# Down products that read their 512 weight columns from two halves in turns

## The reference

```python
u = jax.nn.relu(jnp.einsum('bsd,df->bsf', h2, w_up[l]))
x = x + jnp.einsum('bsf,fd->bsd', u * u, w_down[l])
...
return jnp.einsum('phk,phkd->pd', (gb * hid).astype(xb.dtype), v_tab[eb])
```

## Time and profile before

| | us |
|---|---|
| Median of 2 runs | 3211.09 (3210.66 to 3211.52) |
| Span of the profiled execution, first to last instruction | 3209.0 |
| PE busy (matmul) | 3191.6 |
| PEld busy (weight load) | 2854.0 |
| DVE busy | 2030.1 |
| ACT busy | 1447.3 |

### The profile page before, as it was taken

How to read it: one execution, slowest core, us unless ns; L and a number is a source line. 1 busy time by engine, 2 the same in 40 slices (tenths; PEclk the granted TensorE clock), 3 DMA queues, 4 the chain that set the end, 5 groups by cost and what they waited for, 6 DMA issues and landing times.

```text
span 3209.0 us, 48201 instructions
## 1 busy us (share of the span) xinstructions
PE 3191.6 (99%) x19975; PEld 2854.0 (89%) x19975; DVE 2030.1 (63%) x1837; ACT 1447.3 (45%) x1271; POOL 496.9 (15%) x418
## 2 busy tenths in 40 slices
PE   9999999999999999999999999999999999999999
PEld 7888899999999888888989999999999888888887
DVE  5455665556555667765476888999975555555554
ACT  5454453333433364464444444555544433334333
POOL 0000000000000002136200002888840000000000
PEclk9999999999999999999999999999999999999999
DMA  7444565555555453342255566677676656556563
GB/s 282 165 159 158 172 225 194 196 186 193 195 187 193 158 183 119 132 158 105 93 211 204 199 216 222 224 251 251 229 263 259 241 225 261 228 230 257 226 261 118
DMA packets 129572, 644.18 MB, mean 201 GB/s; under 512 B 12672, under 2 KB 45840, under 8 KB 60304
## 3 DMA queue, kind: packets, MB, share of 16 engines
q1 hardware_dynamic: 95792, 623.03, 53.3%
q10 hardware_dynamic: 33632, 18.99, 1.9%
HBM read 606.31 MB, written 35.66 MB: 200 GB/s over the span
## 4 chain that ended last, share of the span: by engine, by line
PE 97%; DVE 1%; ACT 1%; DMA 0%; SPq 0%; issue 0%; DVEq 0%; ACTq 0%
PE pj L305 12%; PE pj L304 12%; PE pj L306 12%; PE pj L282 7%; PE pj L281 7%; PE pj L280 7%; PE pj L1774 4%; PE pj L1772 4%; PE pj L890 4%; PE pj L892 4%; PE pj L1773 4%; PE pj L891 4%; PE pm L282 2%; PE pt L282 2%; PE pt L281 2%; PE pm L281 2%
## 5 line engine op out<-in xcount | busy, mean ns | idle before, releaser
L262 ACT ACTIVATE hi<-raw 128x2048 fp32r<-128x2048 f32 x534 | 1023.8, 1917 | 1372.7 <-PE pj L306 640.7
L269 DVE TENSOR_TENSOR lo<-raw,hi 128x2048 fp32r<-128x2048 f32 x400 | 918.5, 2296 | 677.5 <-ACT hi L262 676.7
L304 PE MATMUL pj<-xh,hi 128*128 128x256 f32 x3328 | 919.9, 276 | 0.0
L305 PE MATMUL pj<-xl,hi 128*128 128x256 f32 x3328 | 918.8, 276 | 0.0
L306 PE MATMUL pj<-xh,lo 128*128 128x256 f32 x3328 | 918.8, 276 | 0.0
L305 PEld LDWEIGHTS pj<-xl,hi 128*128 128x128 f32 x3328 | 625.0, 188 | 0.6
L304 PEld LDWEIGHTS pj<-xh,hi 128*128 128x128 f32 x3328 | 624.8, 188 | 0.6
L306 PEld LDWEIGHTS pj<-xh,lo 128*128 128x128 f32 x3328 | 624.8, 188 | 0.0
L269 DVE TENSOR_TENSOR lo_in<-raw,hi 128x2048 fp32r<-128x2048 f32 x134 | 308.1, 2300 | 268.9 <-ACT hi L262 268.4
L2495 POOL TENSOR_SCALAR hotA<-cst,slotT 128x128 fp32r<-128x128 f32 x256 | 337.9, 1335 | 462.0 <-ACT slotT L2333 425.4
L1772 PE MATMUL pj<-hi,xh 128*128 128x512 f32 x576 | 232.3, 403 | 0.0
(11 more groups left out here) (408 smaller groups left out, 4243.8 us busy)
## 6 DMA issues: line engine op xcount, KB each, us to landing
raw<-w_peer SPq DMA_DIRECT2D x256, 1024.0 KB, 6.3
raw<-w_mlp SPq DMA_DIRECT2D x128, 1024.0 KB, 4.8
raw<-w_in SPq DMA_DIRECT2D x102, 1024.0 KB, 4.8
raw<-w_out SPq DMA_DIRECT2D x32, 1024.0 KB, 4.8
raw<-w_q SPq DMA_DIRECT2D x16, 1024.0 KB, 4.9
act_scratch<-hidU SPq DMA_DIRECT2D x32, 512.0 KB, 3.0
gates_scratch<-stage ACTq DMA_DIRECT2D x8, 2048.0 KB, 17.5
hidV<-act_scratch SPq DMA_DIRECT2D x32, 512.0 KB, 3.7
```

What stands on the lines that cost most here:

```text
L262: nc.scalar.activation(hi[:, j, :], raw[:, j, :], ACT.Copy).then_inc(hi_ready, 1)
L269: nc.vector.tensor_tensor(low(q)[:, j, :], raw[:, j, :], hi[:, j, :].bitcast(F32), ALU.subtract).then_inc(lo_ready, 1)
L304: nc.tensor.matmul(o, hi[:, j, cols], xh[:, k0 + k, :], start=clears, stop=False, skip_group_check=True)
L305: nc.tensor.matmul(o, hi[:, j, cols], xl[:, k0 + k, :], start=False, stop=False, skip_group_check=True)
```

## The change

The 512 columns of a group of down weights are no longer read in the order of their addresses. The group is seen as two halves of 256 columns (1024 bytes each). A matmul reads `run` columns of the first half, then `run` columns of the second, then the next `run` of the first, and so on. `run` is 4 (16 bytes) in the MLP and 32 (128 bytes) in the experts. The host lays the weights of a group so that the columns, read in this order, come out in the old order; the output is written to the same addresses in the same order as before. The number of DMAs, their sizes, the split into `hi` and `lo`, and the number and shape of the matmuls stay as they are. The up products and the dense products of the two input and output projections are not touched. The argument `k0`, which was always 0 here, goes.

```diff
+MLP_RUN, V_RUN = 4, 32
...
+        def halves(x, run):
+            return x.rearrange("p (h g c) -> p g h c", h=2, c=run)
...
-        def multiply(pe, q, j, pair, sh, sl, k0, first, last):
+        def multiply(pe, q, j, pair, sh, sl, run, first, last):
             pe.wait_ge(lo_ready, q * SLOTS + j + 1)
             for k in range(4):
-                cols = slice(k * NB, (k + 1) * NB)
+                w_h, w_l = (halves(w[:, j, k * NB:(k + 1) * NB], run) for w in (hi, lo))
                 for t in range(TT):
                     tok = slice(t * P, (t + 1) * P)
+                    out = pair[:, t, :].rearrange("p (g h c) -> p g h c", h=2, c=run)
                     begin, end = first and k == 0, last and k == 3
-                    nc.tensor.matmul(pair[:, t, :], sh[:, k0 + k, tok], hi[:, j, cols], start=begin, stop=False)
-                    nc.tensor.matmul(pair[:, t, :], sh[:, k0 + k, tok], lo[:, j, cols], start=False, stop=False)
-                    mm = nc.tensor.matmul(pair[:, t, :], sl[:, k0 + k, tok], hi[:, j, cols], start=False, stop=end)
+                    nc.tensor.matmul(out, sh[:, k, tok], w_h, start=begin, stop=False)
+                    nc.tensor.matmul(out, sh[:, k, tok], w_l, start=False, stop=False)
+                    mm = nc.tensor.matmul(out, sl[:, k, tok], w_h, start=False, stop=end)
             mm.then_inc(pe_used, 1)
...
-                             coef_h[par], coef_l[par], 0, True, True)
+                             coef_h[par], coef_l[par], MLP_RUN, True, True)
...
-                    multiply(pe, s + Q_V, n, v_pair[n], cV_h[par], cV_l[par], 0, first, False)
+                    multiply(pe, s + Q_V, n, v_pair[n], cV_h[par], cV_l[par], V_RUN, first, False)
...
+def in_halves(chunks, run):
+    n = chunks.shape[0]
+    return np.ascontiguousarray(chunks.reshape(n, P, 4, NB // (2 * run), 2, run).transpose(0, 1, 2, 4, 3, 5)).reshape(n, P, CH)
...
-        "w_mlp": ffn_chunks(up_chunks(f(w_up)[0]), down_chunks(f(w_down)[0])),
+        "w_mlp": ffn_chunks(up_chunks(f(w_up)[0]), in_halves(down_chunks(f(w_down)[0]), MLP_RUN)),
...
-                             np.ascontiguousarray(v).reshape(4 * PEER_SB, P, CH)),
+                             in_halves(np.ascontiguousarray(v).reshape(4 * PEER_SB, P, CH), V_RUN)),
```

More of the change, by code:

```diff
@@ L283, in multiply, with multiply_tile @@
+                    nc.tensor.matmul(out, sh[:, k, tok], w_l, start=False, stop=False)
+                    mm = nc.tensor.matmul(out, sl[:, k, tok], w_h, start=False, stop=end)
             mm.then_inc(pe_used, 1)
-        def multiply_tile(pe, q, j, pair, sh, sl, t, end):
+        def multiply_tile(pe, q, j, pair, sh, sl, run, t, end):
             tok = slice(t * P, (t + 1) * P)
+            out = pair[:, t, :].rearrange("p (g h c) -> p g h c", h=2, c=run)
             for k in range(4):
[L289 to L292, removed]
+                w_h, w_l = (halves(w[:, j, k * NB:(k + 1) * NB], run) for w in (hi, lo))
+                nc.tensor.matmul(out, sh[:, k, tok], w_h, start=False, stop=False)
+                nc.tensor.matmul(out, sh[:, k, tok], w_l, start=False, stop=False)
+                mm = nc.tensor.matmul(out, sl[:, k, tok], w_h, start=False, stop=end and k == 3)
@@ L2315, in tail @@
                     pe.wait_ge(v_coef_l, PEER_SB - 1 + b)
-                    multiply(pe, Q_END - 2 + c // 4, c % 4, v_pair[n], cV_h[b], cV_l[b], 0, False, b == 1)
+                    multiply(pe, Q_END - 2 + c // 4, c % 4, v_pair[n], cV_h[b], cV_l[b], V_RUN, False, b == 1)
                 pe.wait_ge(lo_ready, Q_END * SLOTS)
@@ L2320, in tail @@
                         b, n = TAIL_ORDER[c]
-                        mm = multiply_tile(pe, Q_END - 1, c % 4, v_pair[n], cV_h[b], cV_l[b], t, b == 1)
+                        mm = multiply_tile(pe, Q_END - 1, c % 4, v_pair[n], cV_h[b], cV_l[b], V_RUN, t, b == 1)
                         if t == 1:
```

## The result

The change makes the kernel slower: 3273.32 us against 3211.09 us, a ratio of 1.0194 with a 95% interval of 1.0164 to 1.0224. Timed again (e12) the ratio is 1.0194, 1.0177 to 1.0211. That is 62 us more, where 47 us less was forecast, and outside the range of 3150 to 3225; whether it is more than 2% the intervals leave open.

A forecast was written before the change was run, and what follows sets the result against it. TensorE, busy 99% of the span, was taken to bound the kernel; 4608 touched matmuls at 10.15 ns less each give 46.8 us, so 3211.1 - 46.8 = 3164 us, range 3150 to 3225.

The forecast's parts named there:

- The cover: Other engines and DMA beside TensorE: claimed to keep up with stages 5% shorter, new waits of PE costed at nothing.
- the 14 ns: In the touched float32r matmuls: 228.9 ns against 215 for the plain F32 attention scores, taken as avoidable.
- collisions of the two readers: In the down matmuls: the weight load and the moving reader were said to collide, costing 14 ns per matmul.
- the value near rows 7: Down matmuls in the new order: 218.75 ns, near the plain F32 attention scores' 215; 10.15 ns less per matmul.
- two cases: Down matmuls: the forecast gain, 3152 to 3179 us, chance 0.45, and half the effect, 3180 to 3205 us, 0.15.
- the 3.75 ns added to the forecast: Down matmuls: added to 215 ns as what a float32r product shows over plain F32 where the load binds.
- first rival: Down matmuls: the 14 ns are a fixed loss per column of float32r streaming; no effect, 3211 us; chance 0.22.
- The rival that came true: Fetch of the moving operand: each jump costs a column's time, 0.447 ns, 110 us over 245,760 jumps; chance 0.15.
- point of decision: Fetch of the moving operand: above 46.8 us / 245,760 = 0.19 ns per jump the kernel was to be slower.

The follow-up runs named there:

- e12: The change as it is, timed again against the kernel before in three rounds: 3273.31 us, ratio 1.0194.
- e3: Kernel before, old order, each down product loading 32 stationary columns in place of 128: 3220.2 us.
- e5: Changed kernel with the jump between the two stretches over 1280 bytes in place of 1024: 3273.3 us.
- e11: Changed kernel with runs of 64 columns in both the MLP and the experts: 3210.78 us, ratio 1.000.
- e6: Changed kernel with each run of 4 (MLP) or 32 (experts) columns read twice in a row, then the next: 3220.4 us.
- e10: Changed kernel, MLP reading 2 of every 4 columns, experts reading each run of 8 columns twice in a row: 3590.6 us.
- e4: Changed kernel, runs of 4 and 32, each down product loading 32 stationary columns in place of 128: 3252.4 us.
- e8: Changed kernel with runs of 16 columns in the MLP and 64 in the experts: 3239.7 us.
- e1: Changed kernel with the run lengths exchanged, 32 columns in the MLP and 4 in the experts: 3284.0 us.

## Why the prediction was wrong

**What was right.** TensorE sets the end; 4608 matmuls of 512 columns are touched; a nanosecond on each counts in full; nothing else moves. The waits of PE stayed below 15 us. The dense products of the projections stayed at 229 ns (means of 229.3 before and after over the steps under 300 ns). The cover was never tested, because the stages became longer.

**The step that failed** is the one in which the 14 ns over the plain F32 reader became "collisions of the two readers", and with it the value near rows 7. The prediction called it an inference, and then gave it 0.60 of the chance in two cases. e3 refutes it: with the listed load 80 ns shorter the matmul costs 231.1 ns, not 217 to 220. e5 refutes the part about addresses modulo 512 bytes: another remainder changes nothing. In e11 the two halves lie at one remainder as in the change, the runs are free, and none of the 14 ns goes. What stands in its place is e6 and e10. The float32r stream is bound by fetching pieces of 16 bytes, at 1.77 to 1.79 ns each, a little slower than the 215.8 / 128 = 1.69 ns in which four columns pass when a piece costs nothing new. By this account the plain F32 reader of the earlier trace rows is free of the 14 ns because it takes its columns at half the pace and so needs a piece half as often; no run varies the plain product, so this is argued and not shown. The second half of the failure is what the sum left out: the runs themselves, which the forecast put at nothing and which cost 20 to 21 ns per matmul with 4 columns and 7.8 with 32.

Two readings of rows were off as well. The two matmuls of the earlier trace rows are two records of one product: line 686 is run once for each of 8 heads, and the trace has 16. And the operands of the earlier trace rows (`dT`, `dB`) are plain F32 by the code, so the 3.75 ns added to the forecast were not "what a float32r product shows". They moved it by 17 us and not its sign.

The Trainium skill had spoken against the inference, in the rule on two independent read ports that the prediction cited and made its first rival, with 0.22 ("TensorE: Matmul & The Clock Gate", "Step-by-step: what each phase is for"). e3 agrees with it for the old order: a smaller load brings nothing, 231.1 against 228.9 ns. For runs of 32 no run shows it cleanly: in e4 the price falls from 7.8 to 2.2 ns, with a smaller load and a narrower output at once.

**The first rival** was right on what the 14 ns are, a loss of the stream itself, but not on the result. It made the loss one per column; it is one per piece.

**The rival that came true** is the slower one, with 0.15. Its place was right, the fetch of the moving operand. Its price was taken as a column's time, 0.447 ns per jump; measured are 0.16 to 0.49 ns, depending on the run, and 0 with runs of 64. Its reason, that the reader stops at the end of a run, does not hold as it stands: ends that lead back to the piece just read (e6, MLP) or from one piece to the next in ascending order (e10, MLP) are free. Its split was wrong: "Nearly all of it would sit in the MLP", while the MLP's down products lost 33 us and the experts' 24, because a run of 32 pays three times as much per jump as a run of 4. Its point of decision, 0.19 ns per jump, compared a price with a gain that did not exist.

Beside it the prediction cited the rule on lines from the Trainium skill ("SBUF — State Buffer", "Specifications (TRN2)"): lines of 16 bytes, at least two hits per line for full bandwidth, and a penalty for each crossing to a new line. By the two hits, as the prediction took it, a run of 16 bytes has no price, since four float32 hit one line. The runs agree with the 16 bytes and with a penalty for each new line (215.8 ns where each line serves eight columns, 453.2 where it serves two). They do not bear out that two hits are enough: with two hits the matmul costs 453.2 ns, with four in ascending order 228.9, and with four and a jump after each line 249 to 252.

**A term that was missing**: the up products between the MLP's down blocks, 6 us. The prediction said that they stay at 113 ns. In the changed kernel they run at 117.8 ns behind every other down block and at 113.4 behind the rest; in e8 at 117.8 behind all of them, in e1 at 113.5 behind all. Their own code is the same in all these kernels, so their pace depends on how the down products around them read. What sets it was not tried; the blocks also take two coefficient buffers by turns, and no run separates that.

**Open.** Why a run of 64 columns is free when a run of 32 is not, and why the quotient per jump grows up to there. Lengths between 32 and 64 were not tried. Nor is it settled whether a break in the order of addresses is what costs, or the end of a run in the pattern. With runs of 8 read twice (e10) the order breaks 32 times and the matmul costs 240.0 ns, as with the 32 breaks of runs of 16 (e8, 240.1); that speaks for the breaks. With runs of 32 read twice (e6) it breaks 8 times and costs 236.7, as with 16 breaks; that speaks for the ends. A pattern whose runs of 32 columns follow each other in ascending order, with a gap between them, would tell; no run has one.

## What to carry to other kernels

In this kernel a matmul with a moving operand of 512 float32r columns is bound by how many 16-byte pieces it fetches, down to the 215.8 ns that it takes with half as many; runs of 64 columns (256 bytes) cost nothing, and runs of 32 and fewer do, so do not split a row into short runs. When two rows of a trace differ in several things at once (here the type, the pace and the number of pieces), the cheapest test is the one that moves a single one of them. Here that was a load of a quarter of the size, and it would have taken 0.60 of the chance away.

## What the runs showed of the hardware that was not expected

The loss within a stream is the same to 0.1 ns in every stage, although starts alternate: before the change three matmuls in turn cost about 226, 229 and 232 ns, always 687 together. Other patterns have other rounds, and the same instructions can settle in one of two paces: MLP blocks of the changed kernel cost 249.0 and 251.8 ns by turns, and the up products 113.4 or 117.8.

Taking only half of each 16 bytes doubles a matmul of 512 columns, from 228.9 to 453.2 ns, while reading each 16 bytes twice saves 13 ns of it. Shortening the weight load from 188 to 108 ns, with an output of 32 partitions, saves nothing in the old order; it costs 2 ns.
